# A two-block transformer in one program: gate units evacuated by halves, merged chunks shared out over three engines, weight splits ahead of a phase's last evacuation

## The reference, cut to what matters

```python
for l in range(2):                                   # first block, 272 tokens
    h = layer_norm(ALPHA * h + 0.5 * swiglu(h, up1, down1))
    b, c, hh, c_q, c_kv, k_r, g_conv, g_mla = split(h @ w_in)
    y_conv = b * causal_conv3(c * hh)                # width 512
    y_mla  = causal attention of 8 heads from c_q, c_kv, k_r    # width 512
    merged = sigmoid(g_conv + b0) * (y_conv @ w_br_conv) \
           + sigmoid(g_mla  + b1) * (y_mla  @ w_br_mla)
    h = layer_norm(ALPHA * h + merged @ w_o)
    h = layer_norm(ALPHA * h + 0.5 * swiglu(h, up2, down2))
x = h[16:]
for l in range(2):                                   # second block, 256 tokens
    h = rmsnorm(x)
    ...                                              # pooling, mLSTM, forgetting attention
    merged = sig(g0) * (y_pool @ w0) + sig(g1) * (y_ml @ w1) + sig(g2) * (y_fox @ w2)
    x = x + merged @ w_out
    h = rmsnorm(x)
    x = x + (swiglu(h) if l == 0 else top 2 of 8 experts(h))
return rmsnorm(x)
```

## Time and profile before

| | |
|---|---|
| Median of 3 runs | 3004.61 us (3004.44 to 3006.03) |
| The profiled execution's own time | 3001.41 us |
| Its span (first to last instruction) | 2999.6 us |
| Mean granted TensorE clock | 0.971 |
| TensorE busy | 2807.4 us (94%) |
| VectorE busy | 2021.0 us (67%) |
| ScalarE busy | 1662.3 us (55%) |
| GpSimd busy | 592.2 us (20%) |
| Chain of waits | PE 86%, DVE 7%, ACT 3%, issue 2% |
| Memory | 665 MB, 222 GB/s on the mean, 380 to 390 in the experts |

### The profile page before, as it was taken

The page is one execution under the profiler, slowest core; times in us unless marked ns, Lnnn a source line. Parts: engine busy times, 40 slices in busy tenths (PEclk is TensorE's granted clock), DMA queues, the critical chain, the costliest instruction groups (busy, mean ns, idle before and its releaser), DMA issues.

```text
span 2999.6 us, 68093 instructions
## 1 busy us (share of the span) xinstructions
PE 2807.4 (94%) x27812; PEld 2302.6 (77%) x27812; DVE 2021.0 (67%) x1973; ACT 1662.3 (55%) x1711; POOL 592.2 (20%) x449
## 2 busy tenths in 40 slices
PE   7999889989988889979999999998999999999998
PEld 5877567878876668767778887778797897887885
DVE  3456465554555555556675555677989999999986
ACT  4435535445445444345535445635777777777775
POOL 3204002102104012003002103001332332432422
PEclk9999999999999999989999999999999999999999
DMA  8663255657634356634366655346999999999996
GB/s 207 174 190 116 71 169 155 165 161 201 165 124 125 120 150 177 192 94 158 113 175 177 188 175 161 108 156 236 385 378 383 394 378 386 392 377 385 391 383 236
DMA packets 657498, 665.38 MB, mean 222 GB/s; under 512 B 25302, under 2 KB 513116, under 8 KB 657276
## 3 DMA queue, kind: packets, MB, share of 16 engines
q1 hardware_dynamic: 655424, 658.70, 66.9%
q0 software_dynamic: 704, 0.59, 0.3%
q10 hardware_dynamic: 1148, 2.83, 0.2%
HBM read 661.01 MB, written 1.05 MB: 221 GB/s over the span
## 4 chain that ended last, share of the span: by engine, by line
PE 86%; DVE 7%; ACT 3%; issue 2%; DVEq 2%; DMA 1%; ACTq 0%; SPq 0%
PE ps L1752 23%; PE ps L1754 22%; PE ps L1753 22%; PE ps L2351 3%; PE ps L2350 3%; PE ps L2349 3%; DVE w_lo L1087 2%; PE ps L1873 1%; ACT w_hi L649 1%; DMA w<-in_ffn_w_up 1%; PE ps L1879 1%; PE ps L2002 1%; PE ps L2306 1%; PE ps L2063 1%; PE ps L2065 1%
## 5 line engine op out<-in xcount | busy, mean ns | idle before, releaser
L1752 PE MATMUL ps<-x_hi,w_hi 128*128 128x128 f16 (+2 forms) x5856 | 1363.7, 255 | 100.6 <-ACT mix L801 29.6
L1753 PE MATMUL ps<-x_lo,w_hi 128*128 128x128 f16 (+2 forms) x5856 | 1363.2, 255 | 0.0
L1754 PE MATMUL ps<-x_hi,w_lo 128*128 128x128 f16 (+2 forms) x5856 | 1362.5, 255 | 0.0
L1087 DVE SCALAR_TENSOR_TENSOR w_lo<-w,w_hi 128x2048 f16<-128x2048 f32 (+4 forms) x338 | 691.9, 2057 | 333.8 <-ACT w_hi L649 327.5
L1752 PEld LDWEIGHTS ps<-x_hi,w_hi 128*128 128x128 f16 x5856 | 579.0, 99 | 177.6 <-issue 96.1
L649 ACT ACTIVATE w_hi<-w 128x2048 f16<-128x2048 f32 (+4 forms) x338 | 562.7, 1673 | 251.9 <-PE ps L1754 208.5
L1753 PEld LDWEIGHTS ps<-x_lo,w_hi 128*128 128x128 f16 x5856 | 578.9, 99 | 60.8
L1754 PEld LDWEIGHTS ps<-x_hi,w_lo 128*128 128x128 f16 x5856 | 579.2, 99 | 58.6
L1511 DVE SCALAR_TENSOR_TENSOR w_lo<-w,w_hi 128x2048 f16<-128x2048 f32 x224 | 544.5, 2456 | 30.0 <-ACT w_hi L1017 29.7
L1017 ACT ACTIVATE w_hi<-w 128x2048 f16<-128x2048 f32 x224 | 419.0, 1903 | 37.1 <-DMA w<-in_moe_w_down 15.8
L1734 POOL CAST ff<-pb 128x512 f16<-128x512 f32 x56 | 140.2, 2503 | 763.8 <-DVE pb L1592 763.8
(11 more groups left out here) (339 smaller groups left out, 3852.0 us busy)
## 6 DMA issues: line engine op xcount, KB each, us to landing
w<-in_ffn_w_up SPq DMA_DIRECT2D x176, 512.0 KB, 4.9
w<-in_moe_w_gate SPq DMA_DIRECT2D x80, 1024.0 KB, 8.9
w<-in_moe_w_up SPq DMA_DIRECT2D x80, 1024.0 KB, 9.0
w<-in_moe_w_down SPq DMA_DIRECT2D x64, 1024.0 KB, 8.0
w<-in_w_in SPq DMA_DIRECT2D x112, 512.0 KB, 4.6
mix<-in_moe_w_down SPq DMA_DIRECT2D x48, 1024.0 KB, 8.3
w<-in_mix_w_in SPq DMA_DIRECT2D x64, 512.0 KB, 4.8
mix<-in_moe_w_gate SPq DMA_DIRECT2D x32, 1024.0 KB, 9.4
```

Source lines behind the costliest of these rows:

```text
L1087: vec.scalar_tensor_tensor(k.w_lo[:, s, 0:size], k.w32[:, s, 0:size], WS, k.w_hi[:, s, 0:size], ALU.mult, ALU.subtract).then_inc(k.parts_r ...
L1752: pe.matmul(acc, w_hi, x_hi, start=first, stop=False)
L1753: pe.matmul(acc, w_hi, x_lo, start=False, stop=False)
L1754: return pe.matmul(acc, w_lo, x_hi, start=False, stop=last)
```

## The change

It has four parts.

1. **Halves of the side units.** TensorE signals a new semaphore `half_done` behind half 0 and `unit_done` behind half 1 as before; ScalarE takes half 0 one item earlier than before (item m + 4) and half 1 where both stood (item m + 5), each with a signal of its own, and TensorE waits ahead of each half for the same half of the unit before. The phase side counts 18 evacuations instead of 9, and the waits that count them change with it.
2. **The last unit of a phase.** `take_first` is gone: the split for the unit two ahead stands in front of the evacuation of the last unit, as at all other units, in all phases of ScalarE and VectorE that use `over_units_ahead`.
3. **Merged chunks.** VectorE now ends with the sum, which it writes to `prod`, in two buffers (a new semaphore `branches_summed`). ScalarE makes `x_hi` and a float32 copy `merged` of it (in `sq`), each scaled, in `merge`; GpSimd subtracts for `x_lo` (`merge` of its own program). VectorE waits from chunk 2 on for ScalarE's reading of the buffer (`merged_hi`), ScalarE for GpSimd's (`merged_ready`).
4. With it, VectorE's loop over the branch units is written out rather than looped (`loop=False`), the third sum of `take_branch2` is placed in `tmp` and `prod`, one drain between evacuations is moved to the front of the unit, and two drains are gone.

```diff
-    def step(trip, j, q, size, take_first=False):
+    def step(trip, j, q, size):
         g = phase.first + j
-        if take_first:
-            take(trip, j, g, q)
         if size:
             split(g + AHEAD, q, size)
-        if not take_first:
-            take(trip, j, g, q)
+        take(trip, j, g, q)
...
+    def merge(phase, q, done0, t):                    # ScalarE
+        def take(m):
+            act.wait_ge(k.branches_summed, done0 + m + 1)
+            act.activation(k.x_hi[:, m, 0:t], k.prod[:, m % 2, 0:t], ACT.Copy, scale=0.5 * UNW)
+            if m >= 2:
+                act.wait_ge(k.merged_ready, done0 + m - 1)
+            act.activation(k.merged[:, m % 2, 0:t], k.prod[:, m % 2, 0:t], ACT.Copy, scale=0.5 * UNW).then_inc(k.merged_hi, 1)
+        for m in range(KC):
+            late = m + AHEAD - KC
+            split(phase.first + m + AHEAD, q, phase.size if late < 0 else phase.after[late])
+            if m >= 1:
+                take(m - 1)
+        take(KC - 1)
...
-        def take_side(u):
-            unit_used(side.first + u, q)
+        def take_side(u, half):
+            if half:
+                unit_used(side.first + u, q)
+            else:
+                act.wait_ge(k.half_done, l * 9 + u + 1)
...
-                for c in range(2):
-                    n = 2 * (u - 1) + c
-                    a = act.activation(k.mix1[:, 16 + n, :], k.ps[:, c, 0:T1], ACT.Tanh, scale=0.5 * UNW, bias=k.gate_b[:, n:n + 1])
-                a.then_inc(k.act_evac, 1)
+                n = 2 * (u - 1) + half
+                a = act.activation(k.mix1[:, 16 + n, :], k.ps[:, half, 0:T1], ACT.Tanh, scale=0.5 * UNW, bias=k.gate_b[:, n:n + 1])
+            a.then_inc(k.act_evac, 1)
...
-                if n == m + 5:
-                    take_side(u)
+                if n in (m + 4, m + 5):
+                    take_side(u, n - m - 4)
...
         copy_probs(7)
+        take_side(8, 0)
         pair_high(3)
-        take_side(8)
-        ahead_only(S1["branch"], q)
+        take_side(8, 1)
+        merge(S1["branch"], q, l * KC, T1)
...
             m, b = trip * SLOTS + j, 2 * ((j + 1) % 2)
+            vec.drain()
             unit_used(g, q)
...
             vec.drain()
-            vec.tensor_tensor(k.tmp[:, 2:3, :], k.tmp[:, 0:1, :], k.tmp[:, 1:2, :], ALU.add)
-            vec.drain()
-            vec.tensor_scalar(k.x_hi[:, bass.ds(m, 1), :], k.tmp[:, 2:3, :], 0.5 * UNW, None, ALU.mult)
-            vec.drain()
-            vec.scalar_tensor_tensor(k.x_lo[:, bass.ds(m, 1), :], k.tmp[:, 2:3, :], 0.5 * UNW, k.x_hi[:, bass.ds(m, 1), :],
-                                     ALU.mult, ALU.subtract).then_inc(k.merged_ready, 1)
-        over_units_ahead(vec, S1["branch"], q, split, take_branch)
+            if m >= 2:
+                vec.wait_ge(k.merged_hi, l * KC + m - 1)
+            vec.tensor_tensor(k.prod[:, m % 2, :], k.tmp[:, 0, :], k.tmp[:, 1, :], ALU.add).then_inc(k.branches_summed, 1)
+        over_units_ahead(vec, S1["branch"], q, split, take_branch, loop=False)
...
+    def merge(done0, t):                              # GpSimd
+        for m in range(KC):
+            pool.wait_ge(k.merged_hi, done0 + m + 1)
+            pool.tensor_tensor(k.x_lo[:, m, 0:t], k.merged[:, m % 2, 0:t], k.x_hi[:, m, 0:t], ALU.subtract).then_inc(k.merged_ready, 1)
...
-                pe.wait_ge(k.act_evac, act0 + (side.base + u + (1 if u == 0 else 2)))
+            pe.wait_ge(k.act_evac, act0 + (side.base + 2 * u + half + 1))
             a = chain(k.ps[:, half, 0:T1], g % SLOTS, [(kc * 256 + half * P, P, kc) for kc in range(KC)], k.x_hi, k.x_lo)
-            if half == 1:
-                a.then_inc(k.unit_done, 1)
+            a.then_inc(k.unit_done if half else k.half_done, 1)
```

More of the change, by code:

```diff
@@ L116 @@
     ("uv", 1, HEADS1 * VH, "act", 3, False),
-    ("side", 9, UNIT, "act", 9, False),
+    ("side", 9, UNIT, "act", 18, False),
     ("branch", KC, 8 * P, "vec", KC, False),
@@ L222, in over_units_ahead @@
         late = u + AHEAD - phase.units
-        step(u // SLOTS, u % SLOTS, quads + u // SLOTS, phase.size if late < 0 else phase.after[late], take_first=late == AHEAD - 1)
+        step(u // SLOTS, u % SLOTS, quads + u // SLOTS, phase.size if late < 0 else phase.after[late])
 def halves(banks):
@@ L308, in allocate @@
     k.prod = sb("prod", [P, 2, T1], F32)
+    k.merged = k.sq[:, 0:2, :]
     k.tmp = sb("tmp", [P, 3, T1], F32)
@@ L457, in allocate @@
     k.half_grouped = sem("half_grouped")
+    k.half_done = sem("half_done")
+    k.branches_summed = sem("branches_summed")
+    k.merged_hi = sem("merged_hi")
     k.group_parts = sem("group_parts")
@@ L817, in pair_high @@
             act.activation(k.y_hi[:, 1, c, :], k.ps[:, 2 + c % 2, 0:T1], ACT.Copy).then_inc(k.y_hi_ready, 1)
-        take_side(0)
+        take_side(0, 0)
+        take_side(0, 1)
         for n, (h, j) in enumerate(ITEMS1):
@@ L1002, in act_program @@
         take_gated(13)
-        ahead_only(s["branch"], 0)
+        merge(s["branch"], 0, (DEPTH + l) * KC, T2)
         ahead_only(s["wout"], 0)
@@ L1472, in take_branch2 @@
             m, b = trip * SLOTS + j, 2 * (j % 2)
+            vec.drain()
             unit_used(g, q)
             for n in range(3):
-                a = vec.scalar_tensor_tensor(k.tmp[:, n:n + 1, 0:T2], k.mix2[:, bass.ds(m + (24 + 8 * n), 1), :], 1.0,
-                                             k.ps[:, b + n // 2:b + n // 2 + 1, 256 * (n % 2):256 * (n % 2) + 256], ALU.add, ALU.mult)
+                a = vec.scalar_tensor_tensor(k.tmp[:, n, 0:T2], k.mix2[:, m + (24 + 8 * n), :], 1.0,
+                                             k.ps[:, b + n // 2, 256 * (n % 2):256 * (n % 2) + 256], ALU.add, ALU.mult)
             a.then_inc(k.vec_evac, 1)
             vec.drain()
-            vec.tensor_tensor(k.prod[:, 0:1, 0:T2], k.tmp[:, 0:1, 0:T2], k.tmp[:, 1:2, 0:T2], ALU.add)
+            vec.tensor_tensor(k.tmp[:, 0, 0:T2], k.tmp[:, 0, 0:T2], k.tmp[:, 1, 0:T2], ALU.add)
             vec.drain()
-            vec.tensor_tensor(k.prod[:, 1:2, 0:T2], k.prod[:, 0:1, 0:T2], k.tmp[:, 2:3, 0:T2], ALU.add)
-            vec.drain()
-            vec.tensor_scalar(k.x_hi[:, bass.ds(m, 1), 0:T2], k.prod[:, 1:2, 0:T2], 0.5 * UNW, None, ALU.mult)
-            vec.drain()
-            vec.scalar_tensor_tensor(k.x_lo[:, bass.ds(m, 1), 0:T2], k.prod[:, 1:2, 0:T2], 0.5 * UNW, k.x_hi[:, bass.ds(m, 1), 0:T2],
-                                     ALU.mult, ALU.subtract).then_inc(k.merged_ready, 1)
-        over_units_ahead(vec, s["branch"], 0, split, take_branch2)
+            if m >= 2:
+                vec.wait_ge(k.merged_hi, (DEPTH + l) * KC + m - 1)
+            vec.tensor_tensor(k.prod[:, m % 2, 0:T2], k.tmp[:, 0, 0:T2], k.tmp[:, 2, 0:T2], ALU.add).then_inc(k.branches_summed, 1)
+        over_units_ahead(vec, s["branch"], 0, split, take_branch2, loop=False)
         def take_wout(trip, j, g, q):
@@ L1690, in pool_program @@
         pool.tensor_tensor(k.y_lo[:, 0, :, :], c_acc, k.y_hi[:, 0, :, :], ALU.subtract).then_inc(k.conv_ready, 1)
+        merge(l * KC, T1)
         up(S1["up2"], l * L_VEC, T1, k.a_hi1, k.a_lo1)
@@ L1723, in pool_program @@
         a.then_inc(k.pool_ready, 1)
+        merge((DEPTH + l) * KC, T2)
         if l == 0:
```

13 lines of the change are left out of this document (6 added, 7 removed).

## The result

| | before | after |
|---|---|---|
| Median (runs) | 3004.53 us (2998.59 to 3006.03, 4) | 2921.84 us (2919.22 to 2924.14, 4) |
| Profiled execution, span | 3001.41, 2999.6 us | 2921.71, 2919.9 us |
| Mean granted clock | 0.971 | 0.982 |

The ratio is 0.9728, with a 95% interval of 0.9711 to 0.9745: 82.7 us faster. The forecast was 2933, 71.6 faster, with a range of 2914 to 2958.

What follows compares the result with a forecast made beforehand. TensorE, busy 2807.4 of 2999.6 us, was taken as the bound. Waits, splits, chunks and clock (29.2 + 9 + 8.8 + 4.8 + 1.4 + 0.3 + 9.0 + 9) summed to 71.5 us: median 2933, own range 2918 to 2948, 8 in 10 2914 to 2958.

Steps and rivals of the forecast that it cites:

- the up phases and heads: Up phases: a stall too small for a row, counted as 0.3 us in all.
- the tanh pair: Attention loops and their ends: TensorE's waits for ScalarE's tanh go, 22.3 + 6.1 + 0.8 = 29.2 us.
- the layer norms: Six layer norms: mean subtraction starts 1.5 us earlier with the split ahead of the last evacuation, 8.8 us in all.
- narrow unit and gate pair: TensorE's waits behind the narrow unit (2 x 2.42 = 4.8 us) and at the second block's first gate pair (1.4) go.
- the chunks: Branch phases: bound moves from VectorE to TensorE and the next opening starts earlier, 9.0 us in all.
- Next late: What would hold TensorE next: first square after 1.0 us, heads of 8.78, 0.6 at a layer's first wait, openings at 2.7 and 2.0.
- The clock terms: Lower-clock time won back: 9 us in the attention (bounds 0 and 11.2) and 9 elsewhere (-5 and 19).
- The term elsewhere: Clock at layer norms, second block's opening and units behind the narrow one: 9 us, bounds -5 and 19.
- A: Attention: the gate wait only moves, half of 29.2 + 9 is lost, 2952 us; chance 0.13.
- B: Merged chunks: GpSimd's subtraction comes first and VectorE waits; the 9.0 becomes -8.8, 2951 us; chance 0.12.
- C: Gate units: the halves do nothing since weights or scores hold the next unit, 2971 us; chance 0.04.
- D: Phase ends: splits waiting for late weights hold up the last evacuation, slower than before, about 3070 us; chance 0.04.

Runs made afterwards that it cites:

- Experiment 1: Kernel before with one part alone: halves of the side units 2964.81 us, split ahead of the last evacuation 2993.71, merged chunks 2984.20, against 3003.62.
- experiment 3: Changed kernel, but ScalarE takes both halves of a side unit at item m + 5, each with its own signal: 2956.04 us.
- experiments 1 and 5: The second: changed kernel, VectorE taking the last unit ahead of the split in the four branch phases alone, 2915.06 us, or in all its phases, 2930.26 us.
- experiment 7: Kernel before, shifted by 8 extra matmuls of a constant (1.84 us) once, ahead of the first down phase: 3003.19 us.
- experiment 4: Changed kernel, but GpSimd makes each low part of the merged chunks twice, same result: 2927.87 us.
- halves_only: Kernel before with the halves of the side units alone: 2964.81 us against 3003.62.

## Why the prediction was right

**The reading of the waits** held in full. Each term that was read from an idle stretch of TensorE came out within 0.3 us (the up phases and heads, below, were set by guess): the tanh pair (29.2), the layer norms (8.8 against 8.7), narrow unit and gate pair (6.2), the chunks (9.0 against 9.3). Experiment 1 shows for each part that its idling belongs to it, and experiment 3 shows which half of the first edit does the work. "Next late" was right too: a first square after 1.0, heads of 8.78 (8.61), the first wait of a layer at 0.6, openings 2.7 and 2.0 behind the last unit (2.59, 2.15).

**The interplay of the moved split and the chunks**, that the order costs 2.2 at each branch phase and the chunks win it back, is what experiments 1 and 5 show. At these four phases the moved split is a loss (8.5 us of the stages) that the chunks only cover.

**The clock terms** were too small, and account for 7.3 of the 9.3 us that the sum is short: 12.5 for the attention, where I took 9 and my upper bound was 11.2, and 12.8 elsewhere where I took 9. In the attention the clock gave the upper bound itself: 1.66 at each of four heads and 2.23 at each of the two half units are 11.1, all of the 11.2 that stood in the prediction. What goes beyond it is no clock. It is the 0.16 us behind each of the ten waits, which a reading of idling leaves out. The term elsewhere was right only by its wide bounds, and in part by luck: it holds a loss of 1.7 us at each of the two branch openings of the first block, where the clock fell behind waits of 2.6 and had not fallen behind 3.8 and 3.5 before, so other places gave more. The prediction treated it as a sum of prices. The single edits show no such sum: by the medians alone they take away 4, 0 and 3 us of lost clock, together 34. Two traces that agree stage by stage (experiment 7) speak against mere chance in the stages ahead of the experts; but executions of one kernel differ by up to 10 us in time, with the clock. What decides which gap is followed by a fall stays open.

**The up phases** gave 1.4 and the heads of the second block 0.7, where I had 0.3 for the two together: 0.2 to 0.4 in each of seven stages, which I had taken for too small to count.

**Rivals.** A (the gate wait moves) fell: no wait for probabilities came. B fell for this kernel, but its mechanism is real (experiment 4) and has 0.3 us of slack at a chunk. C fell with halves_only, 38.8 us. D had no case: up to the experts only two of ScalarE's splits waited for a load (3.8 us in all), both at the start of the program. Its price was also added up too low (3004.6 + 122 - 47 is 3079, not 3070).

**The range.** The forecast's own range of 2918 to 2948 was worked out from the profiled execution. For the median it is 3 us higher, 2921 to 2951, and the 2921.8 measured lies at its very edge.

## What to carry to other kernels

Idle stretches of the bounding engine, read one by one from what ended them and from what would be late next, add up (54.5 us for three edits alone, 53.8 together). The time that the clock costs did not add up here: give it a range of its own (15 to 20 us over 3000 in this case), and judge an edit by the idling that it removes before its time. Read a clock from more than one execution before you put it down to an edit. A split ahead of an evacuation is right where the splitting engine has slack and wrong where it is the bound; taking the last unit first in those four phases alone is the fastest simple version, 2915 us.

## What the runs showed of the hardware

- The same 20 matmuls behind a gap of 3.82 or 3.83 us ran in 2.42 us at a clock of 1.00 (before) and in 4.48 at 0.50 (halves_only), one execution each.
- Executions of the kernel before had a mean granted clock of 0.968 to 0.973 (15 executions, 2998.0 to 3008.3 us); two traces of nearly the same program (before, shifted) agreed in every stage behind the first attention to 0.02 us, but for 0.07 in the last.
- Each wait that went inside a run of matmuls freed some 0.16 us more than its idling, at a clock of 1.00: heads of 8.61 us against 8.78 of busy time.
- Extra matmuls on an idle TensorE (16 at a norm, filling 3.6 of a wait of 4.24 us) took the lost clock from 53 to 47 us, and the kernel got no faster (2926.3 against 2921.8), as the wait behind the opening grew from 1.25 to 2.92 us.
- A VectorE instruction with two inputs waited for a GpSimd one that had begun 0.26 us earlier: 0.44 became 0.74.
